# Hybrid decoder layer on one core: memory heads of the prompt attention placed ahead of the top-k search, all 17 sample key products on VectorE, and a reordered end

## The reference, cut to what matters

```python
parts = x @ w_in                     # u, cB, cC, q, k, v, qi, ki, wi, qm, and three gates of 1024
conv  = cB * conv3(cC * u)
# prompt: indexer scores (8 heads x 64) -> 64 keys kept for each query -> attention, 8 heads x 64
# sample: indexer scores over 2049 keys -> 256 kept -> keys and values gathered from pages -> attention
mem   = softmax(qm @ mk.T / 8) @ mv  # 4 heads x 64 over 256 memory tokens
m     = g0 * (conv @ w_br_conv) + g1 * (attn @ w_br_attn) + g2 * (mem @ w_br_mem)
h     = LN(alpha * x + m @ w_o)
y     = LN(alpha * h + moe(h))       # 32 gated experts of 256, best group, two experts of it
```

## Time and profile before

| | |
|---|---|
| Median of 3 runs | 604.25 us (602.78 to 604.49) |
| The profiled execution's own time | 603.22 us |
| Its span | 601.3 us, 8683 instructions |
| PE busy | 535.9 us (89%) |
| DVE busy | 279.9 us (47%) |
| ACT busy | 104.7 us (17%) |
| POOL busy | 63.8 us (11%) |
| DMA | 163.53 MB, mean 272 GB/s |
| Chain that ended last, by engine | PE 55%, DMA 19%, DVE 17%, ACT's queue 5% |

### The profile page before, as it was taken

One profiled execution on the slowest core, in us unless ns is written; L12 is line 12 of the kernel. 1 busy time (PEld: TensorE's weight loads), 2 busy tenths in 40 slices (PEclk: granted clock), 3 DMA queues, 4 the chain that ended last, 5 costly groups with the idle time before them and its releaser, 6 DMA issues.

```text
span 601.3 us, 8683 instructions
## 1 busy us (share of the span) xinstructions
PE 535.9 (89%) x3518; PEld 327.6 (54%) x3518; DVE 279.9 (47%) x767; ACT 104.7 (17%) x246; POOL 63.8 (11%) x70
## 2 busy tenths in 40 slices
PE   8999999999999995999899998969999993985770
PEld 4556566565688773777676557524655351521220
DVE  1363766667677687779862597302101100101026
ACT  1001111011310124455200231111111010101021
POOL 0000000001200024488300000000000000000002
PEclk9999999999999996999999999979999998898886
DMA  8981241944443446566989947799999999999951
GB/s 293 399 311 53 87 141 43 375 147 143 140 125 123 141 132 200 177 227 194 328 332 409 334 153 311 267 422 382 422 414 419 421 421 419 422 419 419 417 228 72
DMA packets 47918, 163.53 MB, mean 272 GB/s; under 512 B 5986, under 2 KB 22844, under 8 KB 35844
## 3 DMA queue, kind: packets, MB, share of 16 engines
q1 hardware_dynamic: 39312, 139.81, 60.8%
q0 software_dynamic: 3472, 14.31, 7.1%
q10 hardware_dynamic: 5092, 8.83, 4.2%
HBM read 160.14 MB, written 2.77 MB: 271 GB/s over the span
## 4 chain that ended last, share of the span: by engine, by line
PE 55%; DMA 19%; DVE 17%; ACTq 5%; issue 2%; ACT 1%; SPq 0%; POOLq 0%; POOL 0%; DVEq 0%
PE bank L796 12%; PE bank L605 11%; DMA ring<-in_w_down 10%; PE bank L1159 6%; DMA ring<-in_w_up 5%; PE bank L553 4%; PE bank L1251 3%; ACTq L1516 2%; PE bank L651 2%; DMA proj<-in_w_down 2%; ACTq L1515 2%; PE bank L619 2%; PE bank L1134 2%; PE bank L1116 2%; PE bank L1194 2%
## 5 line engine op out<-in xcount | busy, mean ns | idle before, releaser
L796 PE MATMUL bank<-work,ring 128*128 128x264 f32 x384 | 94.2, 396 | 0.0
L605 PE MATMUL bank<-ring,work 128*128 128x512 f32 (+2 forms) x224 | 91.1, 544 | 0.4 <-DVE work L1746 0.4
L796 PEld LDWEIGHTS bank<-work,ring 128*128 128x128 f32 x384 | 71.2, 192 | 14.8 <-issue 2.8
L1159 PE MATMUL bank<-ring,work 128*32 128x512 f32 x304 | 50.7, 653 | 14.5 <-DMA ring<-in_w_up 11.2
L605 PEld LDWEIGHTS bank<-ring,work 128*128 128x128 f32 x224 | 39.8, 190 | 30.4 <-issue 26.6
L2399 DVE SCALAR_TENSOR_TENSOR work<-work,bank 128x256 f32<-128x256 f32 x8 | 3.4, 422 | 87.5 <-ACT work L1576 87.5
L2411 DVE COPY gates<-bank 128x512 f32<-128x512 f32 x8 | 5.5, 692 | 81.9 <-PE bank L1251 73.2
L1159 PE MATMUL bank<-proj,work 128*32 128x512 f32 x128 | 28.9, 593 | 6.0 <-DMA ring<-in_w_up 3.7
L1251 PE MATMUL bank<-ring,work 128*32 128x512 f32 x176 | 29.6, 664 | 4.5 <-DMA ring<-in_w_down 3.8
L1159 PEld LDWEIGHTS bank<-ring,work 128*32 128x32 f32 x304 | 13.5, 119 | 36.3 <-issue 36.2
L922 PE MATMUL bank<-work,ring 128*128 128x264 f32 x128 | 31.8, 392 | 0.4 <-DVE gates L2137 0.3
(11 more groups left out here) (340 smaller groups left out, 834.7 us busy)
## 6 DMA issues: line engine op xcount, KB each, us to landing
ring<-in_w_up SPq DMA_DIRECT2D x19, 2048.0 KB, 20.1
ring<-in_w_down SPq DMA_DIRECT2D x13, 2048.0 KB, 25.6
ring<-in_w_in SPq DMA_DIRECT2D x21, 1024.0 KB
proj<-in_w_up SPq DMA_DIRECT2D x7, 2048.0 KB, 22.5
misc<-in_w_up SPq DMA_DIRECT2D x5, 1024.0 KB, 25.8
gates<-in_w_up SPq DMA_DIRECT2D x5, 1024.0 KB, 21.1
ring<-in_w_o SPq DMA_DIRECT2D x4, 1024.0 KB, 11.0
proj<-in_w_down SPq DMA_DIRECT2D x2, 2048.0 KB, 24.3
```

The lines of the kernel that those rows point to most:

```text
L605: last = mm(bank[2 * (i % 2) + t][:, 0:w], lhs[:, k, 128 * t:128 * t + 128], rhs[:, k % 4, :], start=(k == 0), stop=(k == KT - 1))
L796: last = mm(b[:, 0:TOK], w[:, k, 128 * (n % 2):128 * (n % 2) + 128], xT[:, k, 0:TOK], start=(k == 0), stop=(k == KT - 1))
L1159: last = mm(bank[5][32 * j:32 * j + 32, :], xTe[q // 2 % 2][:, k, s0:s0 + CAP], up_of(n + j // 2, j % 2, r), start=(k == 0), stop=(k == KT ...
```

## The change

It moves the two memory pairs ahead: their scores are taken during the compaction, their maxima are taken straight from PSUM (`mem_max`; the factor 0.125 goes into the copy of the memory query), their probabilities are turned and used between gate tiles 10 and 14, and gate tiles 15 to 17 come in one row after them. The loop over pairs starts at pair 2. All 17 key rows go through `key_dot` on VectorE, which waits for the gather of each row; GpSimd only issues gathers. At the end the second half of the last down weights is loaded by two DMAs, the products, combines, sums and the norm's steps stand in another order, two products of constants stand between the halves, and VectorE takes two steps of the last quarter over in another form.

The diff, cut to its core:

```diff
-PAIR_TILES = ((15, 16), (17, 18), (19, 20), (21, 22), (23, None), (None, None))
+MEM_PAIRS = NMH // 2
+PAIR_TILES = {2: (18, 19), 3: (20, 21), 4: (22, 23), 5: (None, None)}
-KEY_PRODUCTS = ((), range(0, 3), range(3, 6), range(6, 9), range(9, 12), ())
-KEY_SUMS = ((), (), range(0, 3), range(3, 6), range(6, 9), range(9, 12))
-KEY_DOTS = ((), range(12, 13), range(13, 15), range(15, 17), (), ())
+KEY_DOTS = ((), (), range(0, 4), range(4, 8), range(8, 13), range(13, 17))
+NDOT = 17
...
@@ SyncE @@
                 if n == NU_WO:
-                    sp.wait_ge(kd_mul, NPROD)
                     sp.wait_ge(kd_dot, NDOT)
...
+                    sp.dma_start(d[:, :, 0:512], s[:, :, f, 0:512]).then_inc(quad_in[w], 16)
+                    sp.dma_start(d[:, :, 512:1024], s[:, :, f, 512:1024]).then_inc(tail_in, 16)
...
@@ TensorE, what stands after gate tile 7 @@
+            pe.wait_ge(comp_in, 1)  ...  comp_ps
+            scores(0)
+            gate_tile(8, k1=4)
+            pe.wait_ge(comp_in, 2)  ...  comp_ps
+            gate_tile(8, k0=4)
+            gate_tile(9, k1=2)
+            pe.wait_ge(comp_in, 3)  ...  comp_ps
+            gate_tile(9, k0=2)
+            gate_tile(10)
+            turn(0)
+            turn(1)
+            index_scores(0)
+            gate_tile(11)
+            pe.wait_ge(comp_in, 4)  ...  comp_ps
+            values(0)
+            scores(1)
+            index_scores(2)
+            gate_tile(12)
+            index_scores(4)
+            gate_tile(13)
+            turn(2)
+            turn(3)
+            gate_tile(14)
+            values(1)
+            scores(2)
+            for n in range(15, 18):
+                gate_tile(n)
...
-            for p in range(PAIRS_H):
+            for p in range(MEM_PAIRS, PAIRS_H):
                 turn(2 * p)
                 turn(2 * p + 1)
                 if p + 1 < PAIRS_H:
                     scores(p + 1)
...
@@ TensorE, the last down product @@
+                products(0, 0)
+                products(0, 1).then_inc(used_w, 1)
+                for _ in range(2):
+                    mm(bank[5][:, :], ident, h3[:, 0, 0:512], start=True, stop=True)
+                unit_there(n + 1)
+                products(1, 0).then_inc(y_half, 1)
+                pe.wait_ge(y_act, QUADS)
+                combine_end(0, 0)
+                pe.wait_ge(tail_in, 16)
+                products(1, 1).then_inc(used_w, 1)
+                combine_end(1, 0)
+                pe.wait_ge(y_dve, QUADS)
                 combine_samples(q)
+                combine_end(0, 1)
+                combine_end(1, 1)
...
@@ ScalarE @@
+            exps(0)
+            gate_out(8)
+            exps(1)
+            normalise(0)
+            normalise(1)
+            gate_out(9)
+            gate_out(10)
+            turned_probs(0)
+            turned_probs(1)
             index_relu(0)
             index_relu(1)
             gate_out(11)
             index_relu(2)
             index_relu(3)
+            gate_out(12)
+            exps(2)
             index_relu(4)
+            exps(3)
             gate_out(13)
+            normalise(2)
             index_relu(5)
+            normalise(3)
+            turned_probs(2)
+            turned_probs(3)
+            for n in range(14, 18):
+                gate_out(n)
+            exps(4)
+            exps(5)
+            normalise(4)
+            normalise(5)
...
@@ GpSimd @@
-            def key_product(i):
...
             for p in range(1, PAIRS_H - 1):
                 pool.wait_ge(at_t, 2 * p + 1)
+                for i in VALUE_GATHERS[p]:
+                    value_gather(i)
...
@@ VectorE @@
             def key_dot(i):
+                if i < 16:
+                    dve.wait_ge(kg_in[i % 2], 16 * (i // 2 + 1))
...
+            def mem_max(n):
+                dve.wait_ge(at_s, n + 1)
...
+                link(V.tensor_reduce(st[:, 0:2], score_bank(n)[:, :].rearrange("p (t n) -> p t n", t=2), AX.X, ALU.max,
+                                     negate=True), at_m)
...
+                if i == 1:
+                    head_out(0)
                 if i == 2:
+                    mem_max(2)
                 if i == 3:
+                    mem_max(3)
                 if i == 4:
+                    inverse(2)
                 if i == 5:
+                    inverse(3)
+            for i in range(INDEX_ROUNDS[-1][1], 2 * TOPP // 8):
+                topk_round(i)
+            head_out(1)
+            softmax(4)
+            softmax(5)
+            inverse(4)
+            inverse(5)
+            for p in range(MEM_PAIRS, PAIRS_H):
                 if p + 1 < PAIRS_H:
                     softmax(2 * p + 2)
                     softmax(2 * p + 3)
+                dots = list(KEY_DOTS[p])
                 for part in (0, 1):
+                    key_dot(dots[part])
                     if p + 1 < PAIRS_H:
                         inverse(2 * p + 2 + part)
                 if p + 1 < PAIRS_H:
                     head_out(p)
+                for i in dots[2:]:
+                    key_dot(i)
                 if p == PAIRS_H - 2:
                     dve.wait_ge(act_gate, NT)
                     merge(0)
                     merge(1)
...
@@ VectorE, the end @@
+            y_rstd(0, 4)
+            y_scale(0, 0, y_ready)
             y_rstd(2, 6)
+            y_shift(2, mean_s, stats[:, 55:56], n1_ready)
+            y_centre(0, 1)
+            y_scale(0, 1, y_ready)
+            y_centre(1, 1)
+            y_scale(1, 1, y1b_ready)
```

More of the change, by code:

```diff
@@ L781, in gate_hook, with gate_tile @@
                 hooks[0] += 1
-            def gate_tile(n, then=None, part=None):
+            def gate_tile(n, then=None, k0=0, k1=KT):
                 b = bank[gate_bank(n)]
-                if part == 1:
+                if k0:
                     pass
@@ L792, in gate_tile @@
                 w = slot(unit_slot(u)).rearrange("p (k n) -> p k n", k=KT)
-                if n % 2 == 0 and part != 1:
+                if n % 2 == 0 and k0 == 0:
                     pe.wait_ge(unit_sem(u), UC[u])
-                for k in range(4 * (part == 1), 4 if part == 0 else KT):
+                for k in range(k0, k1):
                     last = mm(b[:, 0:TOK], w[:, k, 128 * (n % 2):128 * (n % 2) + 128], xT[:, k, 0:TOK],
@@ L858, in scores @@
                             last.then_inc(at_s, 1)
-            gate_tile(10)
-            index_scores(0)
-            gate_tile(11)
-            pe.wait_ge(comp_in, 4)
-            for g in range(NPG):
-                for j in range(4):
-                    last = mm(bank[7][32 * j:32 * j + 32, 384:416], Alo4[:, j, g, :],
-                              Ahi4[:, j, g, :], start=(g == 0), stop=(g == NPG - 1))
-            last.then_inc(comp_ps, 1)
-            gate_tile(12)
-            index_scores(2)
-            scores(0)
-            gate_tile(13, part=0)
-            index_scores(4)
-            gate_tile(13, part=1)
             def turn(n):
@@ L931, in _ @@
                 ahead, behind = PAIR_TILES[p]
-                if p == 0:
-                    gate_tile(14, part=1)
                 if ahead is not None:
@@ L1295, in _ @@
                     combine(q - 1)
-                down(q)
-            combine_last(QUADS - 1)
+                if q < QUADS - 1:
+                    down(q)
+            down_last()
             def more(it):
@@ L1442, in _ @@
             sample_exp(0, NMH, 16)
-            for n in range(4, 11):
+            for n in range(4, 8):
                 gate_out(n)
@@ L1698, in _ @@
                 pool.wait_ge(at_t, 2 * p + 1)
-                products, gathers = list(KEY_PRODUCTS[p]), list(VALUE_GATHERS[p])
-                for i in range(4):
-                    value_gather(gathers[i])
-                    if i < len(products):
-                        key_product(products[i])
+                for i in VALUE_GATHERS[p]:
+                    value_gather(i)
             pool.wait_ge(m_ready, KT)
@@ L2082, in _ @@
             link(V.tensor_copy(sgnd[:, 0:128], posi))
+            inverse(0)
+            inverse(1)
             io = c("iota")[:, 0:16].unsqueeze(1).broadcast_to([128, 128, 16])
@@ L2446, in _ @@
                 dve.wait_ge(more_c, 1)
+                dve.wait_ge(comb, QUADS + 3)
                 for t in range(2):
```

204 lines of the change are left out of this document (81 added, 123 removed).

## The result

The changed kernel takes 611.8 us in the median (610.05 to 612.95), the kernel before 603.5 beside it: a ratio of 1.0155, with a 95% interval from 1.0123 to 1.0187. Run once more beside other kernels it gave 1.0166 (1.0136 to 1.0196). It is slower, by more than I forecast: 610.5 over 604.25 would be 1.010 (6.2 us; it is 8.3 us between these medians).

What follows compares the result with a forecast made beforehand. TensorE's order of work bounds up to about 390 us, then the stream of expert weights. Stretch 5.6 + clock 2.6 − end 2.0 = 6.2 us slower, from 604.25 to 610.5 us; range 604.5 to 614.0.

Steps and rivals of the forecast that it cites:

- The front: Up to the last memory transpose: waits of 4.7 and 1.8 us stay, transpose ends at 236.9; gain 1.4 us.
- The wait at head 4: New TensorE wait of 3.3 us at `turn(4)`, as ScalarE's `exps(4)` stands behind `gate_out(17)`; head 5 another 0.4.
- VectorE's queue: From pair 3's scores at 260.1, softmaxes, seventeen rows and the rest take 37.8 us, to 297.9.
- The wait ahead of the sample maximum: TensorE stands still 4.3 us ahead of `sample_max`, which comes at 298.0 instead of 292.25.
- the two at the branch products: TensorE waits of 0.6 and 0.5 us at the branch products, for the last three gate copies and `merge(0)`.
- moving the products costs about 1 us net: Twelve products cost VectorE 8.7 us, against 3.6 saved on scalings and reductions and about 4 from GpSimd collisions.
- The clock: TensorE's clock falls behind both new waits, together 2.6 us; bounds 0 and 5.7; a fall may vary between executions.
- SP and POOL: W_o's loads, now waiting for row 16, are issued at 297.2, 13.0 us ahead of the mark: no cost.
- The end: Last down products to last store: 2.0 us gained, bounds 0 and 4; last combine at 585.4 instead of 586.5.
- The sum: Whole kernel: 5.6 + 2.6 − 2.0 = 6.2 us slower, 610.5 us on the median; chance 0.46.
- that the pairs overlap: Rival: VectorE starts rows early, waits at `turn(4)` and `sample_max` vanish, 599.8 us; chance 0.12.
- that the stream swallows the delay: Rival: DMA bounds from `sample_values`' end on, so only the end's gain counts, 602.3 us; chance 0.08.

Runs made afterwards that it cites:

- kernel 9: Experiment 4's kernel with gate tiles 14 and 15 moved ahead of the transposes of heads 2 and 3: 598.3 us, ratio 0.9925 to the kernel before.
- Experiment 1: Changed kernel with ScalarE's exponentials and scalings of heads 4 and 5 behind gate tile 14's copy instead of tile 17's: 608.5 us, 1.0102 to the kernel before.
- experiment 2: Changed kernel with key rows 0 to 5 moved on VectorE ahead of the reciprocals of heads 4 and 5, ScalarE's order unaltered: ratio 1.0055 to the kernel before.
- experiment 3: Changed kernel with ScalarE's exponentials moved earlier and six key rows early on VectorE, row 0 ahead of the two reciprocals: ratio 1.0014 to the kernel before.
- experiment 4: Experiment 3's kernel with the later key rows dealt out four, four and three, none behind the last two branch tiles: 598.5 us, 0.9944 to the kernel before.
- experiment 6: Changed kernel with 12 of 17 key rows' products given back to GpSimd, VectorE keeping their sums and five rows: ratio 1.0068 to the kernel before.
- experiment 8: Kernel before with only the new end: 0.9995; the same without its two products of constants: 0.9956.
- experiment 10: Experiment 4's kernel without the constants: 597.5 us, 0.9916; then kernel 9 without them, three rows early, the rest dealt anew: 593.0 us, 0.9820.
- experiment 5: Changed kernel run once more without any edit: 613.6 us, ratio 1.0166 to the kernel before.

## Why the prediction was right, and where it was not

*The front.* I had the last memory transpose end at 236.9, with waits of 4.7 and 1.8. They are 4.53 and 1.61; the transpose ends at 237.6, 0.5 of it from ahead of the stretch. That the heads' move does not close these waits was right: kernel 9 closed them by putting work there.

*The wait at head 4.* 3.3 us forecast, 3.01 measured, released by the line named, with VectorE idle for 9.07 us where I had nearly 10. Experiment 1 shows its cause. The 0.4 for head 5 did not come.

*VectorE's queue.* 37.8 us from 260.1 to 297.9; measured 260.14 to 298.11. The wait ahead of the sample maximum is 4.30 as forecast, the two at the branch products 0.57 and 0.51 against 0.6 and 0.5. Experiments 2, 3, 4 and 6 show that the place of the rows makes this wait. The step that said that moving the products costs about 1 us net was right as a sum of work, not as a price: its 3.6 us of savings belong to the heads' move. Measured against the same order of heads with products on GpSimd (experiment 6), it costs 5 to 6 us.

*The clock: the first mis-sized term.* I took 2.6 us for two falls of 1.3. From the sample maximum to `sample_values` it was 8.4 us before (292.25 to 300.64) and is 11.1 after, so the second fall alone costs 2.7. The first did not come in the profiled execution and cost 1.2 in the other trace of the same kernel. Together they are 3.9. That 2.6 met the 2.7 of the profiled execution was luck: one fall twice as dear, and the other not there. The lower fall that I took from the earlier trace rows was too small for the second wait, behind which the clock stood at half for 6 us. Why so long is not shown; before, the same steps ran at 1.00. I also argued that my two waits were longer than all that left the clock alone (0.8). That misread the old trace: in it TensorE waits 3.68 us ahead of 499.43, and the clock is 1.00 in every 2 us row from 494 to 506. The forecast that the same wait may meet a fall in one execution and not in the other was borne out; by the Trainium skill (TensorE: Matmul & The Clock Gate, Part 1) the chip looks at instants that don't depend on the kernel, and the two traces agree with that, though they can't prove it.

*SP and POOL.* No cost, as said.

*The end: the second.* 2.0 us forecast, 1.0 measured. The sum had the last combine 1.1 us earlier, and VectorE's last step about 1.7 us earlier. Laid from the second transposes ahead of the group (574.31 before, 582.23 after) to the last combine's end it is 12.2 us both times: the 2.10 us wait and the half clock are gone, and the constants (1.98) and the copy's 0.72 have come. The constants' own time was in my sum and came out right (until 579.0; 579.1 in the old trace's times). Mis-sized was what stands behind them: the copy took 0.72 and not 0.6, and products and combines that I had at 0.8 to 0.9 took 1.0 to 1.1 each from start to start, which makes up the 1.1 us. VectorE's chain then ends as far behind the first 16 products as before (21.3 and 21.4 us), and so does the issue of the last store (22.9 and 22.8), which I had 1.9 us earlier. Only the sample rows' chain on GpSimd ends earlier, by 1.1 us; that the 1.0 us gained comes from it is likely and not shown. My own figures had the half load there at 576.8, before the constants start at 577.2, and I did not ask what the constants were then for; experiment 8 shows that there was no wait left for them to fill.

*The sum.* 6.2 forecast, 6.9 in the profiled spans: 5.4 for the stretch without the clock (5.6), 2.7 for the clock (2.6), 0.5 from ahead of the stretch and −0.7 made up in the expert stage, neither of which I had, and −1.0 for the end (−2.0). The medians differ by 8.3. Part of that is that the clock can fall at head 4 as well, 1.2 us in the one other execution with a trace; the rest is open, since the other executions have none. Of the rivals, that the pairs overlap (599.8, a ratio of 0.9926) needed what experiments 1 to 4 put in by hand, and came to 0.9944 there; that the stream swallows the delay is excluded but for 0.7 us, since 7.9 of 8.6 us reached the last group, and in the same experiments time gained in this stretch arrived at the end.

## What to carry to other kernels

When work is handed from one engine to another, count not only its sum but the queue position of each piece: six of 17 rows, moved into a gap, were worth 6 us (experiment 2), and in experiment 9 six rows there were too many: they took back part of what two gate tiles had brought, and with three the kernel was faster (experiment 10). Before moving a chain ahead, look in every in-order queue for what stands in front of its next link; here the copy of a gate tile held two exponents for 8 us, and with them VectorE for 9.1 and TensorE for 3.0. And take filler work out once by itself: what was put in to cover a wait may be the path after the wait has gone.

## What was not expected of the hardware

- A wait's length did not decide whether TensorE's clock fell. Behind the same 3.01 us it stayed at 1.00 once and fell three times (experiments 2, 5 and 6); behind 1.8 us ahead of the sample maximum it was 0.50 from 300 to 302 in experiment 2 and from 294 to 296 in experiment 3, and 1.00 in experiment 6; behind 3.68 us in the expert stage of the kernel before it stayed at 1.00. Behind 4.3 us ahead of the sample maximum it fell in all three traces that have that wait.
- In two traces VectorE began an instruction late, with no releaser named on the core: in experiment 1, 2.4 us after the scores were done, behind 10.37 us of idle time, and in experiment 9 a copy at 274.31, 1.9 us after the products it reads, behind 2.36 us. It isn't explained here.
